# Transposes between the products, gates on the way out of PSUM, squares and residual by column groups

## The reference

```
mod = c @ w_ada + b_ada                              # 6 x 2048: shift1, scale1, gate1, shift2, scale2, gate2
h = rmsnorm(x, g_pre_mix) * (1 + scale1) + shift1
proj = h @ w_in                                      # q, k, v, the recurrence's inputs, gate_a, gate_h
y_a = sliding_window_attention(...) @ w_attn_proj
y_h = (rmsnorm(hgrn2_recurrence(...)) * sigmoid(g_h)) @ w_hgrn_proj
merged = sigmoid(gate_a) * y_a + sigmoid(gate_h) * y_h
x = x + gate1 * rmsnorm(merged @ w_out, g_post_mix)
h = rmsnorm(x, g_pre_ffn) * (1 + scale2) + shift2
x = x + gate2 * rmsnorm((silu(g) * u) @ w_ffn_out, g_post_ffn)      # g, u = split(h @ w_ffn_in)
```

```
h = rms_norm(x, norm_mix_w);  x = x + concat(y_a, y_g) @ w_out        # attention and gated linear attention
h = rms_norm(x, norm_ffn_w);  x = x + (gelu(u_gate) * u_val) @ w_ffn_down
h = rms_norm(x, norm_ple_w);  x = x + sigmoid(h @ w_ple_gate) * (p @ w_ple_proj)
return rms_norm(x, final_norm_w)
```

## Time and profile before

| | |
|---|---|
| median of 3 runs | 2954.57 us (2954.3 to 2956.34) |
| the profiled execution | 2956.99 us, of it 2955.2 us from the first to the last instruction |
| busy | PE 2797.1, DVE 1788.7, ACT 1275.1, POOL 238.8 us |
| DMA | 588.59 MB, 199 GB/s over the span |
| mean granted TensorE clock | 0.975 |

### The profile page before, as it was taken

How to read it: one execution, slowest core, us unless ns; L and a number is a source line. 1 busy time by engine, 2 the same in 40 slices (tenths; PEclk the granted TensorE clock), 3 DMA queues, 4 the chain that set the end, 5 groups by cost and what they waited for, 6 DMA issues and landing times.

```text
span 2955.2 us, 45353 instructions
## 1 busy us (share of the span) xinstructions
PE 2797.1 (95%) x17746; PEld 2532.8 (86%) x17746; DVE 1788.7 (61%) x1937; ACT 1275.1 (43%) x1463; POOL 238.8 (8%) x163
## 2 busy tenths in 40 slices
PE   4899999998699999999997999998999999999998
PEld 4798887787599998899986989876999988999876
DVE  7876778687854446544466443555566654666545
ACT  2256553333444443333334443533555533444354
POOL 2010121100000100001100000100112100122000
PEclk8899999999899999999998998999999999999999
DMA  9975546587835556655475542445355555545553
GB/s 359 341 265 190 204 146 218 213 307 275 292 130 184 185 198 243 242 185 184 172 255 192 181 155 87 149 152 171 132 186 183 185 192 192 185 171 182 187 180 119
DMA packets 297929, 588.59 MB, mean 199 GB/s; under 512 B 12234, under 2 KB 17342, under 8 KB 296926
## 3 DMA queue, kind: packets, MB, share of 16 engines
q1 hardware_dynamic: 293496, 578.03, 56.4%
q10 hardware_dynamic: 4326, 9.09, 0.9%
HBM read 584.98 MB, written 2.10 MB: 199 GB/s over the span
## 4 chain that ended last, share of the span: by engine, by line
PE 84%; DVE 10%; issue 2%; ACT 2%; DMA 1%; POOL 0%; DVEq 0%; ACTq 0%; POOLq 0%; SPq 0%; PEldq 0%
PE psum L761 14%; PE psum L765 14%; PE psum L763 14%; PE psum L750 12%; PE psum L754 12%; PE psum L752 12%; DVE mod_acc L619 3%; DVE ada_acc L833 3%; DVE w_lo L708 2%; PE bank L889 1%; PE bank L2270 1%; ACT w_hi L696 1%; ACT junk L966 0%; DMA raw<-in_w_out_dram 0%; PE bank L887 0%
## 5 line engine op out<-in xcount | busy, mean ns | idle before, releaser
L708 DVE TENSOR_TENSOR w_lo<-raw,w_hi 128x1024 fp32r<-128x1024 f32 x916 | 1191.6, 1316 | 1016.7 <-ACT w_hi L696 1007.9
L696 ACT ACTIVATE w_hi<-raw 128x1024 fp32r<-128x1024 f32 x916 | 951.4, 1047 | 1433.4 <-PE psum L754 653.9
L761 PE MATMUL psum<-h_hi,w_hi 128*128 128x256 f32 x3392 | 961.2, 283 | 1.0 <-PE bank L629 0.7
L765 PE MATMUL psum<-h_hi,w_lo 128*128 128x256 f32 x3392 | 959.9, 283 | 0.0
L763 PE MATMUL psum<-h_lo,w_hi 128*128 128x256 f32 x3392 | 959.9, 283 | 0.0
L761 PEld LDWEIGHTS psum<-h_hi,w_hi 128*128 128x128 f32 x3392 | 651.2, 192 | 2.4 <-issue 2.1
L763 PEld LDWEIGHTS psum<-h_lo,w_hi 128*128 128x128 f32 x3392 | 651.2, 192 | 0.0
L765 PEld LDWEIGHTS psum<-h_hi,w_lo 128*128 128x128 f32 x3392 | 651.1, 192 | 0.0
L750 PE MATMUL psum<-w_hi,h_hi 128*128 128x512 f32 (+1 forms) x928 | 365.8, 394 | 12.4 <-DVE w_lo L708 3.8
L754 PE MATMUL psum<-w_hi,h_lo 128*128 128x512 f32 (+1 forms) x928 | 361.9, 390 | 0.0
L752 PE MATMUL psum<-w_lo,h_hi 128*128 128x512 f32 (+1 forms) x928 | 361.7, 390 | 0.0
(11 more groups left out here) (322 smaller groups left out, 2096.4 us busy)
## 6 DMA issues: line engine op xcount, KB each, us to landing
raw<-in_w_in_dram SPq DMA_DIRECT2D x120, 1024.0 KB, 5.0
raw<-in_w_ffn_in_dram SPq DMA_DIRECT2D x88, 1024.0 KB, 4.8
raw<-in_w_ffn_up_dram SPq DMA_DIRECT2D x88, 1024.0 KB, 4.8
raw<-in_w_ada_dram SPq DMA_DIRECT2D x64, 1024.0 KB, 5.1
raw<-in_w_ffn_out_dram SPq DMA_DIRECT2D x44, 1024.0 KB, 5.0
raw<-in_w_ffn_down_dram SPq DMA_DIRECT2D x44, 1024.0 KB, 5.1
ada_raw<-in_w_ada_dram SPq DMA_DIRECT2D x64, 512.0 KB, 7.8
raw<-in_w_out_dram SPq DMA_DIRECT2D x32, 1024.0 KB, 5.1
```

Source lines behind the costliest of these rows:

```text
L696: nc.scalar.activation(w_hi[:, slot, :, 0:ncol], raw[:, rs, 2 * h:2 * h + 2, 0:ncol], ACT.Copy).then_inc(split_hi, inc)
L708: nc.vector.tensor_tensor(w_lo[:, slot, :, 0:ncol], raw[:, rs, 2 * h:2 * h + 2, 0:ncol], w_hi[:, slot, :, 0:ncol].bitcast(F32), ALU.subtra ...
L761: pe.matmul(o, fh, hi[:, k, :], start=first and f % 2 == 0, stop=False, skip_group_check=True)
L765: mm = pe.matmul(o, fl, hi[:, k, :], start=False, stop=last, skip_group_check=True)
```

## The change

1. `mix_gate` and `mix_out` are no loops any more but groups 21 to 26 and 27 to 30 of `mix_in`, so the PSUM areas go on alternating. The 48 modulation units are spread anew: groups 4 to 20 carry 26 of them (20 before), the gate groups 12 as before, the `w_out` groups 10 (16 before).
2. The merged tiles are transposed in three pieces: 8 tiles after the first half of group 26, 4 after its second half, 4 after the first third of group 27.
3. `norm1` to `norm4`: PE transposes the first four pairs, then alternates one half of the next stage's first group with one pair (`normed_products`).
4. The gate is multiplied as a group leaves PSUM (`w_out`) or, in `down1`, as its sum is complete; the row sums stand before the last two halves of a group.
5. Squares are taken by groups of 512 columns as these are finished, and added up by a small DVE reduction; the residual is eight `scalar_tensor_tensor` of 512 columns that write `x` directly, and the squares of `x` follow piece by piece.

```diff
-        self.mix_in = Phase(self, 1, [None] * 4 + [full] * 7
-                            + [full, half] * (D // COLS) + [full, half],
-                            mod=[0] * 4 + [2, 2, 2, 1, 1, 2, 2] + [0, 0, 0, 0, 2, 1, 2, 1, 2, 0])
-        self.mix_gate = Phase(self, D // COLS - 1, [full, half], mod=[3, 1])
-        self.mix_out = Phase(self, D // COLS // 2, [full, full], mod=[4, 4])
+        self.mix_in = Phase(self, 1, [None] * 4 + [full] * 7
+                            + [full, half] * (2 * D // COLS) + [full] * (D // COLS),
+                            mod=[0] * 4 + [2] * 7 + [1, 0, 1, 1, 2, 1, 2, 1, 2, 1]
+                            + [3, 1] * 3 + [3, 3, 3, 1])
...
+        def normed_products(pe, ph, stage, r, transposed=False):
+            for b in range(4):
+                transpose_pair_pe(pe, stage, x, b, r)
+            for h in range(KD // 2):
+                products(pe, ph, 0, 0, h_hi, h_lo, transposed=transposed, ready=stage, part=(h, h + 1))
+                if h < 4:
+                    transpose_pair_pe(pe, stage, x, 4 + h, r)
...
+        def part_squares_act(act, r, src, sums, c):
+            for t in range(TT):
+                nc.scalar.activation(junk[:, t * COLS:(t + 1) * COLS], src(t), ACT.Square,
+                                     accum_out=sums[:, t, c]).then_inc(sem(f"part_squares{r}"), 1)
+                act.wait_ge(sem(f"part_squares{r}"), TT * PART[r] + t + 1)
...
+        def part_sums_dve(dve, r, sums):
+            dve.wait_ge(sem(f"part_squares{r}"), TT * D // COLS)
+            nc.vector.tensor_reduce(stats[:, r, 0:2], sums, AX_X, ALU.add).then_inc(sem("squares"), 2)
...
         def residual_dve(dve, chain, r):
             dve.wait_ge(sem("rms"), r + 1)
-            for t in range(TT):
-                chain(nc.vector.scalar_tensor_tensor(tokbuf[:, t, :], tokbuf[:, t, :],
-                                                     stats[:, r, 2 + t:3 + t], gate_row[:],
-                                                     ALU.mult, ALU.mult))
-                ins = nc.vector.tensor_tensor(x[:, t, :], x[:, t, :], tokbuf[:, t, :], ALU.add)
-                ins.then_inc(sem("x_ready"), 1)
+            for c in range(D // COLS):
+                for t in range(TT):
+                    part = slice(c * COLS, (c + 1) * COLS)
+                    nc.vector.scalar_tensor_tensor(x[:, t, part], tokbuf[:, t, part], stats[:, r, 2 + t:3 + t],
+                                                   x[:, t, part], ALU.mult, ALU.add
+                                                   ).then_inc(sem("x_ready"), 1)
+            part_sums_dve(dve, r + 1, part_sq[:, 1])
...
@@ ACT, down1, second part (mix_out2 and down2 have the same lines for x)
+                        else:
+                            act.wait_ge(psum_free[g], ph.freed(i, g))
+                            for t in range(TT):
+                                nc.scalar.activation(junk[:, t * COLS:(t + 1) * COLS],
+                                                     tokbuf[:, t, bass.ds(i * 2 * COLS + g * COLS, COLS)],
+                                                     ACT.Square, accum_out=part_sq[:, 0, t, bass.ds(i * 2 + g, 1)]
+                                                     ).then_inc(sem("part_squares3"), 1)
+                            act.wait_ge(sem("part_squares3"), 2 * (2 * i + g + 1))
...
@@ DVE, the w_out groups
+                    if g > 26 and at == (g, 2):
+                        c = g - 27
+                        part_ = slice(c * COLS, (c + 1) * COLS)
+                        dve.wait_ge(sem("part_squares1"), 2 * (c + 1))
+                        dve.wait_ge(bank_free[3], emptied(f"mod_in{8 + c}", 3))
+                        nc.vector.tensor_tensor(tokbuf[:, :, part_], psum[ph.pair[g]][:],
+                                                gate_row[:, part_].unsqueeze(1).to_broadcast([P, TT, COLS]),
+                                                ALU.mult).then_inc(psum_free[ph.pair[g]], 1)
...
@@ DVE, down1, second part
                             nc.vector.tensor_tensor(y, y, psum[g][:], ALU.add).then_inc(psum_free[g], 1)
+                            dve.wait_ge(sem("part_squares3"), 2 * (2 * i + g + 1))
+                            if g == 1:
+                                dve.wait_ge(bank_free[3], emptied("mod_down1", 3, i))
+                            nc.vector.tensor_tensor(
+                                y, y, gate_row[:, bass.ds(i * 2 * COLS + g * COLS, COLS)].unsqueeze(1)
+                                .to_broadcast([P, TT, COLS]), ALU.mult).then_inc(sem("y_gated"), 1)
```

More of the change, by code:

```diff
@@ L348, in turns @@
 @contextmanager
-def turns(eng, n):
-    if n == 1:
-        yield 0
+def turns(eng, n, first=0):
+    if n == first + 1:
+        yield first
     else:
-        with eng.Fori(0, n) as i:
+        with eng.Fori(first, n) as i:
             yield i
@@ L653, in mod_pe @@
                 o = bank[:, 3, :]
-                sum_pe(pe, mod_acc[place_][:, b, :], o, g0 not in (12, 17)
+                sum_pe(pe, mod_acc[place_][:, b, :], o, not 12 <= MOD_COLUMNS[mod_of(ph)][n] < 20
                        ).then_inc(bank_full[3], 1)
@@ L1889, in _ @@
-            split_dve(dve, "merged", h_hi, h_lo, KD)
-            dve.wait_ge(bank_free[3], emptied("mod_gate", 3, 2))
-            modulate_dve(1)
-            ph = plan.mix_out
-            with turns(dve, ph.iters) as i:
-                for g in range(2):
-                    split_w_lo(dve, ph, i, *span(ph, g))
-                    if g == 0:
-                        dve.wait_ge(sem("mix_gain_full"), 16)
-                    mod_dve(dve, ph, i, g)
-            dve.wait_ge(bank_free[3], emptied("mod_out", 3, 3))
+                    if at == (20, 1):
+                        dve.wait_ge(sem("mix_gain_full"), 16)
@@ L2193, in _ @@
             nc.gpsimd.tensor_tensor(first, first, part_b[:], ALU.add).then_inc(sem("merged_sum"), 1)
-            ph = plan.mix_gate
-            with turns(pool, ph.iters) as i:
-                pool.wait_ge(psum_free[1], ph.freed(i, 1))
-                now = tokbuf[:, :, bass.ds((i + 1) * COLS, COLS)]
+            for n in range(1, 4):
+                g = 20 + 2 * n
+                pool.wait_ge(psum_free[plan.mix_in.pair[g]], plan.mix_in.freed(0, g))
+                now = tokbuf[:, :, n * COLS:(n + 1) * COLS]
                 nc.gpsimd.tensor_tensor(now, now, part_b[:], ALU.add).then_inc(sem("merged_sum"), 1)
@@ L2378, in _ @@
             pe.wait_ge(sem("mirror_ready"), 1)
-            for g in range(len(ph.groups)):
+            normed_products(pe, ph, "norm2", 4, transposed=True)
+            for g in range(1, len(ph.groups)):
                 for s, part in enumerate(parts(ph, g)):
@@ L2382, in _ @@
                     if g < 13:
-                        products(pe, ph, 0, g, h_hi, h_lo, transposed=g < 4 or g in (6, 7),
-                                 ready="norm2" if g == 0 else None, part=part)
+                        products(pe, ph, 0, g, h_hi, h_lo, transposed=g < 4 or g in (6, 7), part=part)
                     else:
@@ L2443, in _ @@
             pe.wait_ge(sem("normed"), 8)
-            transpose_pe(pe, "norm3", x, KD, 5)
+            normed_products(pe, plan.up2[0], "norm3", 5, transposed=True)
             for part, (g0, n) in enumerate(FFN_PARTS):
                 ph = plan.up2[part]
-                with turns(pe, ph.iters) as i:
+                if part == 0:
+                    products(pe, ph, 0, 1, h_hi, h_lo, transposed=True)
+                with turns(pe, ph.iters, 1 - part) as i:
                     for g in range(2):
-                        products(pe, ph, i, g, h_hi, h_lo, transposed=True,
-                                 ready="norm3" if g == 0 and part == 0 else None)
+                        products(pe, ph, i, g, h_hi, h_lo, transposed=True)
                 if part == 1:
@@ L2475, in _ @@
             pe.wait_ge(sem("normed"), 10)
-            transpose_pe(pe, "norm4", x, KD, 6)
-            for g in range(len(plan.ple.groups)):
-                products(pe, plan.ple, 0, g, h_hi, h_lo, ready="norm4" if g == 0 else None)
+            normed_products(pe, plan.ple, "norm4", 6)
+            for g in range(1, len(plan.ple.groups)):
+                products(pe, plan.ple, 0, g, h_hi, h_lo)
 _INS = ["x", "c", "positions", "w_ada", "b_ada", "g_pre_mix", "g_post_mix", "g_pre_ffn",
```

280 lines of the change are left out of this document (154 added, 126 removed).

## The result

The changed kernel takes 2965.45 us (median of 6 runs, 2963.77 to 2968.86); in the same session the kernel before took 2956.04 (6 runs, 2954.3 to 2958.4). The ratio is 1.0033, 95% interval 1.002 to 1.0046: about 9 us slower. The forecast was 2925, with a range up to 2941.

The account below looks back on a forecast made before the run. The prediction took PE to be the bound, through its instructions and its standstills, mainly waits for norm diagonals. Gains less the 4.0 us cost summed to 29.6 us off 2956.99, 2927.4, forecast as 2925 for the median; range 2915 to 2941.

Parts of the forecast that it names:

- The interleave: Norms: products alternating with transposes fill PE's waits for banks in norm1; gain 1.9 us, bounds 0 to 3.
- Rival 5: Norms: the exchange fails as an interleave, PE waiting for every bank; 2933 us, chance 0.03.
- Groups 4 to 20: Six more modulation units on DVE and one more column sum on PE cost 4 us, bounds 1 to 20.
- rival 1: Groups up to 20: the front cannot hold six more units, 15 us more than the 4; 2940 us, chance 0.14.
- Ahead of norm2: Gap from PE's last product to norm2: shorter chain to the diagonal gains 3.9 us, net 2.9 after 1.0 for down1.
- PSUM area: After group 20: alternating areas remove PE's 3.7 us wait and the low clock behind it; gain 5.4 us.
- merge: Merged tiles transposed in three pieces: less waiting and full clock, with a 1.2 us stall left; gain 8.6 us.
- mix_out: The w_out groups: less DVE work per group makes PE the bound, 91.2 us instead of 96.9; gain 5.7 us.
- the gap ahead of norm1: From PE's last product to norm1: squares and residual in 512-column pieces, 14.6 us instead of 20.4; gain 5.8.
- Norm3: Wait ahead of norm3, 9.2 us before: cheaper squares gain 2.1 us.
- Rivals 2 and 3: Group-end waits and costlier 512-column pieces, 2939 us, chance 0.11; ACT held at eight group ends, lead lost, 2967, chance 0.05.
- Rival 4: Merged tiles' transposed pieces: low clock through them and the first products behind, 7 us; 2932 us, chance 0.03.

Follow-up runs that it names:

- plain_norms: Changed kernel with all eight pairs of a norm transposed before the products, as in the kernel before; 2945.22 us, ratio 0.995 to the kernel before.
- split_order: Changed kernel, position-table wait moved later, ACT and DVE splitting the weights of half 4 + h just ahead of the norm's pair 4 + h; 2931.36 us, ratio 0.9906.
- front_before: Changed kernel with groups 4 to 20 given the 20 units and five sums of before, groups 21 to 26 three units each; 2969.94 us.
- toep_late: Changed kernel with PE's waits for the position table and mirror matrix moved behind norm2's transposes and first group; 2959.19 us, ratio 1.0005.
- before_again: The kernel before, unchanged, one execution for a second profile; 2959.29 us.
- spread: split_order with 20 units up to group 20, four and one per pair of groups 21 to 26, four in the first three w_out groups; 2920.76 us.
- front_24: split_order with one unit instead of two in groups 7 and 8, and four instead of three in groups 21 and 25; 2931.03 us.
- plain_toep: Changed kernel with both edits, those of toep_late and plain_norms; 2934.74 us, ratio 0.9923.

## Why the prediction was wrong

1. **The interleave** (forecast: gain 1.9; it cost 20.2 by the medians of `plain_norms`, 24.5 by the ratios). The failed step is "products can fill these waits ... No matmul is added": it counted PE's instructions alone. In the kernel before, ACT and DVE have all eight pairs behind them at 829 us and split the weights of half 4 next, while PE is still in its first two halves. Once pair 7 comes behind product half 3, those weights come behind it too, and the lead of four halves is used up exactly there. `split_order` shows it: same order on PE, no wait. None of the rivals said this. Rival 5 had PE wait for every bank; it waited for no bank, but for weights.
2. **Groups 4 to 20** (cost 4 forecast, 12.8 measured, 12.5 of them back in `front_before`). The failed step is the choice "I take 4, near the idle rows". The idle time of 1.4 us at each half lies between splits of weights, where DVE runs four halves ahead. The units were put where PE has no lead over DVE: ahead of `fac`, of the softmax's maxima, which ACT's exponentials wait for, and with these the next `w_hi`. This is rival 1 (15 more than 4, chance 0.14) at 9 more; the bound of 20 held.
3. **Ahead of norm2** (4.9 less forecast in the gap, of which the moved row sum is 1.0; 3.3 more measured). The chain to the diagonal was right (16.9 against 17.3, and 17.0 of wait in `toep_late`). The failed step is the path: PE's start was taken from the diagonal alone, and the wait for `toep_full`, which changed places with the transposes, was left out. It decides because the table is issued late and takes 9.5 us. It cost 8.1 us of wait, and 6.3 us of the time by the medians.
4. **The start** (0 forecast, 2.4 measured): not in the forecast, real by `before_again`, cause open.
5. **Right.** PSUM area, merge, `mix_out` and the gap ahead of norm1 were to give 25.5 and gave 26.4: 13.9 for the first two together (14.0), 5.7 for `mix_out` (5.7), 6.7 ahead of norm1 (5.8), with 0.63 for the 1.2 us of stall and 91.1 for the 91.2 us of `w_out`. Norm3 gave 2.3 (2.1), and one wait of 1.09 ahead of norm4 is gone. Rivals 2 and 3 did not come: PE's list of waits has none for weights at a group's end in the `w_out` groups or in `down1`, whose four waits are 0.3 us each and behind row sums, and the charge of 1.0 in `down1` was not needed. That 2965 lies near rival 3's 2967 is chance. Of `mix_out`'s reason, `spread` shows only part: with four units again its `w_out` groups take 94.3 us (681.76 to 776.05) against 92.8, so by these profiles the fewer units were worth about 1.5 of the 5.7, and what gave the rest (the sum's place, the earlier leads, the last group's single unit) was not taken apart.
6. **Rival 4**, the clock in short pieces of transposes, did not come: the three pieces took 1.91, 1.03 and 1.09 us, and the granted clock was 1.00 in 687.5 to 689.6, 694.5 to 697 and 704.5 to 707 us. The rule in the Trainium skill (TensorE: Matmul & The Clock Gate, Part 4: PE-mode transpose), that transposes do not count as busy for the clock, changed nothing at this length among products. The pairs in norm1 (1.06 us each, clock 1.00 from 808 to 822 us) are products with a diagonal and no transposes of that kind, so they say nothing on the rule; behind the waits at the norms the clock fell.

The misses sum to 2.4 + 8.8 + 8.2 (norm2's gap) and 6.4 + 4.6 + 7.1 + 5.1 in the four stretches behind norms, 42.6 us; less 0.9 and 0.2 that came beyond the forecast elsewhere, these are the 41.5 between -29.6 and +11.9.

## What to carry to other kernels

When one engine's order is changed, write down the new order of every engine that feeds it or follows it, and ask for each prefetched buffer when its refill is now issued: here a lead of four halves was used up, since the refill stood behind pairs that PE transposed only after its fourth half. Price a filler by what stands right behind it on its engine and who waits for that, and not by the engine's idle share: the same six units cost 12.5 us in one place and 0.9 in another. And go through moved waits like moved instructions; a wait put ahead of work that doesn't need it costs what its transfer has left, 8.1 us here.

## What the runs showed of the hardware

After a wait of PE of 5.4 us the clock stood at 0.50 for 5.7 us (828.86 to 834.60). With hardly a gap ahead of them (PE busy 4.85 of 5.00 us), the five microseconds from 285 on had 0.66:

```profile
280.00:285.00 5.00, 4.85 (x39) 4.56 (x38) 2.23 (x15) 2.70 (x13) 0.00 (x0) 1.00 0.70 231
285.00:290.00 5.00, 5.00 (x15) 3.98 (x16) 3.01 (x3) 4.98 (x10) 0.00 (x0) 0.66 0.01 3
```

What PE did just before is 24 records of matmuls of 64 columns (281.17 to 283.8) and a column sum, 8 records of one column (283.80 to 284.80). The five profiles without a column sum at this place (two of the kernel before, `front_24`, `front_before`, `spread`) have 1.00 from 275 to 295 us. Of the five with it, the changed kernel and `plain_norms` have 0.66 from 285 on, `split_order` 0.81 and 0.85 in the ten microseconds from 280 on, `toep_late` and `plain_toep` 1.00. So the sum goes with the drop but isn't enough for it; what else it takes is not known.

A square of 512 columns with its sum takes ACT 0.63 to 0.75 us from SBUF (2057.33 to 2057.96; 794.24 to 794.99) and 0.70 from PSUM (789.50 to 790.20), the read-out of 0.19 included, and a multiply-add of 512 columns from SBUF takes DVE 0.67 (8 in 5.39). ACT's load of a table (1.28 us) ahead of `w_hi` lay between the norm and the loop of `up1`; with the first turn ahead of the loop (`split_order`) it comes at 831.81, ahead of the activation, and PE waits for nothing.
